# Neighbourhood bias loaded as one laid-out tensor, a new order of loads and splits in the conditioning, and a mixer without the two long reciprocals

## The reference

```
sh_a, sc_a, g_a, sh_f, sc_f, g_f = split(silu(c) @ w_ada + b_ada)     # the same for c_ctx
h, hc   = rms(x) * (1 + sc_a) + sh_a, rms(ctx) * (1 + csc_a) + csh_a
q, k, v, u, vs = h @ w_in;   kc, vc = hc @ w_in[:, 512:1536]          # q, k normalised per head
s_win   = q . k_window * scale + rpb[head, key row - row + 7, key column - column + 15]
s       = concat(s_win, q . kc * scale);  o = softmax(s) @ (v_window, vc)
x       = x + g_a * (concat(rms(o), rms(sgu(u, vs))) * gain) @ w_out
x       = x + g_f * mixture_of_experts(x)
```

```
r, i    = sigmoid(gates of xb)
log_a   = 8 * r * log_sigmoid(lam);   a = exp(log_a)
mult    = sqrt(-expm1(2 * log_a))                                     # = sqrt(1 - a * a)
h_t     = a_t * h_(t-1) + mult_t * (i_t * xb_t)
p       = softmax(concat(scores + band bias, sink))                   # a head's row
```

## Time and profile before

| | |
|---|---|
| median of 3 runs (2688.72 to 2693.19) | 2691.13 us |
| the profiled execution: its own time | 2688.06 us |
| the profiled execution: its span | 2685.8 us |
| PE busy, share of the span | 2486.6 us, 93% |
| DVE, ACT, POOL busy | 53%, 38%, 4% |
| mean granted clock of PE | 0.968 |
| conditioning | 0 to 46 us |
| projection | 46 to 220 us |
| heads of the first mixer, from the first maxima | 1247.6 to 1299.2 us |
| heads of the second mixer | 2199.6 to 2254.4 us |

### The profile page before, as it was taken

One profiled execution on the slowest core, in us unless ns is written; L12 is line 12 of the kernel. 1 busy time (PEld: TensorE's weight loads), 2 busy tenths in 40 slices (PEclk: granted clock), 3 DMA queues, 4 the chain that ended last, 5 costly groups with the idle time before them and its releaser, 6 DMA issues. The chain is left out here.

```text
span 2685.8 us, 33498 instructions
## 1 busy us (share of the span) xinstructions
PE 2486.6 (93%) x12262; PEld 2056.9 (77%) x12262; DVE 1428.8 (53%) x2063; ACT 1014.8 (38%) x1466; POOL 98.2 (4%) x115
## 2 busy tenths in 40 slices
PE   6887877999969999997899999999999987999998
PEld 3765856888768888785798888888888856988886
DVE  4676667999843332487653332523323777633324
ACT  5325535777722232244433222322222345322221
POOL 0241001000010000000000000000000000000000
PEclk8997988999979999999999999999999998999999
DMA  5974278999752333240233332423323312323322
GB/s 220 320 262 157 89 282 291 409 403 404 313 180 79 101 94 94 86 113 32 63 98 98 94 97 94 122 72 95 100 94 102 90 55 63 95 78 95 100 94 71
DMA packets 313412, 389.55 MB, mean 145 GB/s; under 512 B 15530, under 2 KB 228170, under 8 KB 313316
## 3 DMA queue, kind: packets, MB, share of 16 engines
q1 hardware_dynamic: 301272, 346.15, 38.8%
q0 software_dynamic: 9024, 33.03, 3.4%
q10 hardware_dynamic: 3020, 9.07, 0.8%
HBM read 354.04 MB, written 41.96 MB: 147 GB/s over the span
## 5 line engine op out<-in xcount | busy, mean ns | idle before, releaser
L1652 DVE TENSOR_TENSOR w_part_lo<-w_raw,w_part_hi 128x1024 fp32r<-128x1024 f32 x252 | 308.3, 1225 | 734.0 <-ACT w_part_hi L1648 733.3
L1656 PE MATMUL PS<-xT_hi,w_part_hi 128*128 128x512 f32 (+1 forms) x1472 | 555.9, 378 | 17.5 <-PEq L1924 8.3
L1648 ACT ACTIVATE w_part_hi<-w_raw 128x1024 fp32r<-128x1024 f32 x252 | 266.5, 1060 | 789.8 <-PE PS L1658 755.2
L1657 PE MATMUL PS<-xT_lo,w_part_hi 128*128 128x512 f32 (+1 forms) x1472 | 554.3, 377 | 0.0
L1658 PE MATMUL PS<-xT_hi,w_part_lo 128*128 128x512 f32 (+1 forms) x1472 | 554.1, 376 | 0.0
L1656 PEld LDWEIGHTS PS<-xT_hi,w_part_hi 128*128 128x128 f32 x1472 | 279.0, 190 | 71.1 <-DVE w_part_lo L1652 19.9
L1658 PEld LDWEIGHTS PS<-xT_hi,w_part_lo 128*128 128x128 f32 x1472 | 278.9, 189 | 50.3
L1657 PEld LDWEIGHTS PS<-xT_lo,w_part_hi 128*128 128x128 f32 x1472 | 279.1, 190 | 49.2
L1656 PE MATMUL PS<-w_part_hi,h_hi 128*128 128x512 f32 x576 | 228.2, 396 | 0.0
L1657 PE MATMUL PS<-w_part_lo,h_hi 128*128 128x512 f32 x576 | 227.9, 396 | 0.0
L1658 PE MATMUL PS<-w_part_hi,h_lo 128*128 128x512 f32 x576 | 227.9, 396 | 0.0
(11 more groups left out here) (479 smaller groups left out, 4116.6 us busy)
## 6 DMA issues: line engine op xcount, KB each, us to landing
expert_w_raw<-in_w SPq DMA_DIRECT2D x136, 512.0 KB, 7.2
w_raw<-in_ffn_w_gate SPq DMA_DIRECT2D x88, 512.0 KB, 3.8
w_raw<-in_ffn_w_up SPq DMA_DIRECT2D x88, 512.0 KB, 3.9
w_raw<-in_ffn_w_down SPq DMA_DIRECT2D x88, 512.0 KB, 3.8
w_raw<-in_w SPq DMA_DIRECT2D x68, 512.0 KB, 6.4
w_raw<-in_w_in SPq DMA_DIRECT2D x56, 512.0 KB, 5.4
late_raw<-in_w_ada SPq DMA_DIRECT2D x32, 512.0 KB, 11.5
w_raw<-in_w_out SPq DMA_DIRECT2D x24, 512.0 KB, 5.0
```

What stands on the lines that cost most here:

```text
L1648: nc.scalar.activation(t.hi, raw[t.n % 4], ACT.Copy).then_inc(w_hi, 1)
L1652: nc.vector.tensor_tensor(t.lo, raw[t.n % 4], t.hi.bitcast(f32), ALU.subtract).then_inc(w_lo, 1)
L1656: nc.tensor.matmul(out, a[0][a_at], b[0][b_at], start=first, stop=False, skip_group_check=True)
L1657: nc.tensor.matmul(out, a[0][a_at], b[1][b_at], start=False, stop=False, skip_group_check=True)
```

## The change

1. The bias table comes in as a tensor `rpb_windows`, laid out by query and key outside the kernel, and one DMA of 3 MB on POOL's queue loads it into `nbt`, after the second group's result is out of PSUM. The padded rows, the shifted copies and the 24 reads are gone. The 8 additions of the mask stay.
2. In the conditioning the first 2 MB of `w_ada` are loaded ahead of x. ACT's scaling of x moves behind the first two pieces, and PE's early transposes behind the fourth.
3. Tiles 0 and 1 of `w_in` are split at the end of the conditioning instead of the start of the projection.
4. PE's first product waits for two chunks of x instead of four, and goes block by block.
5. In the mixer, mult is made from a: ACT squares a, DVE makes (a² + 1) tanh(t) in one instruction in head 1, and ACT takes its square root next to the one of the convolution's norm. 1 - a² equals (1 + a²) tanh(t), with a = exp(-t). The scan, the product with the gate and the last split of the recurrence each stand one head earlier. POOL has one product left.
6. The sink's part of the row maximum: a copy and one TENSOR_SCALAR a head are gone from DVE; ACT's exponential adds the sink as its bias.

```diff
@@ -226,8 +222,9 @@
         @block.sync
         def _(sp):
             sp.dma_start(c2[:, :, :], A["cT"]).then_inc(s_c, 16)
-            sp.dma_start(xtok[:, :, :], A["x"][0].rearrange("(b p) d -> p b d", p=P)).then_inc(s_x, 16)
             for i, (q0, q1) in enumerate(ADA_LOADS):
+                if i == 1:
+                    sp.dma_start(xtok[:, :, :], A["x"][0].rearrange("(b p) d -> p b d", p=P)).then_inc(s_x, 16)
                 sec, k0 = q0 // KC, q0 % KC
                 sp.dma_start(wada[:, q0:q1, :], A["w_ada"][0, k0 * P:(k0 + q1 - q0) * P, sec * D:(sec + 1) * D].rearrange("(k p) n -> p k n", p=P)).then_inc(s_aw[i], 16)
...
+            act.dma_start(out_gT[:, :], A["out_gainT"]).then_inc(s_in, 16)
...
             nc.scalar.activation(ssum[:, 0:TB], ssum[:, 0:TB], ACT.Sqrt, bias=eps6[:, 0:1], scale=1.0 / D).then_inc(s_rt, 1)
-            act.wait_ge(s_rpb, 16)
-            act.dma_start(rpad_rows.rearrange("h (r w) -> (h r) w", w=RP), rpad[:, :]).then_inc(s_rpr, 16)
-            act.wait_ge(s_rt, 2)
-            for b in range(2):
-                nc.scalar.activation(xn[:, b, :], xtok[:, b, :], ACT.Copy, scale=ssum[:, b:b + 1]).then_inc(s_xn, 1)
             for q in pieces:
                 p = q - WHOLE
+                if p == 2:
+                    act.wait_ge(s_rt, 2)
+                    for b in range(2):
+                        nc.scalar.activation(xn[:, b, :], xtok[:, b, :], ACT.Copy, scale=ssum[:, b:b + 1]).then_inc(s_xn, 1)
                 act.wait_ge(s_aw[load_of(q)], 16)
                 if p >= 4:
                     act.wait_ge(a_used, p - 3)
                 nc.scalar.activation(a_whi[:, p % 4, :], wada[:, q, :], ACT.Copy).then_inc(a_hi, 1)
                 if q == KC + 1:
                     rows_out(0)
+            split_hi(Tile(0))
+            split_hi(Tile(1))
             rows_out(1)
...
+            split_lo(Tile(0))
+            split_lo(Tile(1))
...
                     nc.tensor.matmul(PS[0:4, rows_bank[0] + h, :], sc4[:, q, :], wada[:, q, h * HALF:(h + 1) * HALF], start=q == 0, stop=False, skip_group_check=True)
-            pe.wait_ge(s_xn, TB)
-            pe.wait_ge(s_in, 48)
-            for c in EARLY:
-                for b in range(TB):
-                    nc.tensor.transpose(PS[:, c, b * P:(b + 1) * P], xn[:, b, c * P:(c + 1) * P], ident[:, :])
...
+                if q == KC - 1:
+                    pe.wait_ge(s_xn, TB)
+                    pe.wait_ge(s_in, 48)
+                    for c in EARLY:
+                        for b in range(TB):
+                            nc.tensor.transpose(PS[:, c, b * P:(b + 1) * P], xn[:, b, c * P:(c + 1) * P], ident[:, :])
...
-            for h in range(8):
-                each = bass.AP(rpad_rows.tensor, h * NDR * RP, [[0, NB_ROWS], [0, QCOLS], [1, NDR * RP]])
...
-            for h in range(8):
-                for kind, off in enumerate((0, -8, -16)):
-                    skew = bass.AP(skewed.tensor, h * (P + 1) * SKEW + 7 * RP + GRID - 1 + off, [[SKEW, P], [RP, NB_ROWS], [1, WCOLS]])
-                    pool.dma_start(nbt[:, h, kind * WIN:(kind + 1) * WIN].rearrange("p (k c) -> p k c", c=WCOLS), skew).then_inc(s_tab, 16)
+            pool.wait_ge(evac1, 2)
+            pool.dma_start(nbt[:, :, :], A["rpb_windows"]).then_inc(s_tab, 16)
...
-            pool.wait_ge(s_tab, 16 * 25)
+            pool.wait_ge(s_tab, 32)
...
-            pe.wait_ge(rd1, 4)
...
                 src, nb = (XT, TB) if g < NCOL else (HC, CB_)
-                for kk in range(2):
-                    kc = 2 * kp + kk
-                    for b in range(nb):
+                for b in range(nb):
+                    if n == 0 and b >= 2:
+                        pe.wait_ge(rd1, b + 1)
+                    for kk in range(2):
+                        kc = 2 * kp + kk
...
-                    pool.drain()
-                    nc.gpsimd.tensor_scalar(i_g[:, :, :], th[:, :, :], 1.0, None, ALU.add).then_inc(m["divisor"], 1)
+                    pool.wait_ge(m["gates_out"], l + 1)
+                    nc.gpsimd.tensor_tensor(xc[:, :, :], xc[:, :, :], i_g[:, :, :], ALU.mult).then_inc(m["gated_in"], 1)
...
-                    last.then_inc(m["tanh_out"], 1)
+                        nc.scalar.activation(sig[:, ch, :], r_g[:, ch, :], ACT.Exp, scale=lamc[:, ch, 6:7])
+                    act.drain()
+                    nc.scalar.activation(r_g[:, :, :], sig[:, :, :], ACT.Square).then_inc(m["tanh_out"], 1)
...
-                            nc.scalar.activation(esink[:, u % 4, :], smax[:, u % 2, :], ACT.Exp)
+                            nc.scalar.activation(esink[:, u % 4, :], nmax[:, u % 2, :], ACT.Exp, bias=sink_l[:, u:u + 1])
...
-                        if u == 3:
-                            act.wait_ge(m["mult_sq"], l + 1)
-                            nc.scalar.activation(th[:, :, :], th[:, :, :], ACT.Sqrt).then_inc(m["mult_out"], 1)
                         if u == 2:
                             act.wait_ge(m["var_done"], l + 1)
                             nc.scalar.activation(xb[:, 0, 0:SEQ], PS[:, 7, :], ACT.Sqrt, bias=eps[:, 0:1]).then_inc(m["std_out"], 1)
...
+                        if u == 2:
+                            act.wait_ge(m["mult_sq"], l + 1)
+                            nc.scalar.activation(th[:, :, :], th[:, :, :], ACT.Sqrt).then_inc(m["mult_out"], 1)
+                        if u == 5:
                             act.wait_ge(m["scan_out"], l + 1)
...
-                        V.tensor_copy(row_sink[:, u % 2:u % 2 + 1], sink_l[:, u:u + 1])
...
-                        V.tensor_scalar(nmax[:, u % 2, :], mx, row_sink[:, u % 2:u % 2 + 1], -1.0, ALU.max, ALU.mult)
-                        dve.drain()
-                        V.tensor_scalar(mx, nmax[:, u % 2, :], row_sink[:, u % 2:u % 2 + 1], None, ALU.add)
+                        V.tensor_scalar(nmax[:, u % 2, :], mx, sink_l[:, u:u + 1], -1.0, ALU.max, ALU.mult)
...
-                            dve.wait_ge(m["divisor"], l + 1)
-                            V.reciprocal(i_g[:, 0, :], i_g[:, 0, :])
-                        elif u == 2:
-                            V.reciprocal(i_g[:, 1, :], i_g[:, 1, :])
-                            dve.drain()
-                            V.scalar_tensor_tensor(th[:, :, :], th[:, :, :], 2.0, i_g[:, :, :], ALU.mult, ALU.mult).then_inc(m["mult_sq"], 1)
-                        elif u == 4:
+                            dve.wait_ge(m["tanh_out"], l + 1)
+                            V.scalar_tensor_tensor(th[:, :, :], r_g[:, :, :], 1.0, th[:, :, :], ALU.add, ALU.mult).then_inc(m["mult_sq"], 1)
+                        elif u == 3:
                             dve.wait_ge(m["mult_out"], l + 1)
+                            dve.wait_ge(m["gated_in"], l + 1)
                             V.tensor_tensor(xc[:, :, :], xc[:, :, :], th[:, :, :], ALU.mult)
                             dve.drain()
                             for ch in range(2):
                                 V.tensor_tensor_scan(th[:, ch, :], sig[:, ch, :], xc[:, ch, :], 0.0, ALU.mult, ALU.add)
                             dve.drain()
-                        elif u == 5:
+                        elif u == 4:
                             V.tensor_tensor(xc[:, :, :], th[:, :, :], gb[:, :, :], ALU.mult).then_inc(m["scan_out"], 1)
-                        elif u == 7:
+                        elif u == 6:
                             dve.wait_ge(m["y_hi"], l * 5 + 1)
...
+    A["rpb_windows"] = c(np.stack([rows[:, 7 + kr - qr, GRID - 1 + off + kc - qc].reshape(8, P, WIN) for off in (0, -8, -16)], 2).transpose(1, 0, 2, 3).reshape(P, 8, 3 * WIN))
```

30 lines of the change are left out of this document (7 added, 23 removed).

## The result

The changed kernel takes 2661.51 us (median of 4 runs, 2659.99 to 2665.99) against 2692.16 us of the kernel before in the same comparison (4 runs, 2688.72 to 2693.23). The ratio, worked out over all of these runs, is 0.9891, with a 95% interval of 0.9874 to 0.9908: 29 us or 1.1% less (the two medians lie 30.7 us apart). The forecast was 2661, from a sum of 28.6.

What follows compares the result with a forecast made beforehand. PE was taken to bound most of the program, with gains only where it waits. Terms 17 + 4.6 + 7 = 28.6 us gave 2659.5 from the profiled execution, 2662.5 from the median, stated as 2661; range from one below 2649 to 2676.

Steps and rivals of the forecast that it cites:

- the exchange of the loads: Conditioning: w_ada's first 2 MB ahead of x starts PE's whole products 5.2 us sooner, but only 0.4 us comes through.
- The projection, -17: Projection: without the bias copies' DMA traffic, 17 us of the 19.6 us lost waiting for weight tiles come back.
- the 2.7 us left for POOL's additions: Projection: POOL's 8 mask additions still slow DVE's work beside them, so 2.7 us of the loss stays.
- The loss of 19.6: Projection: the stretch of 16 tiles takes 112.5 us against 92.9 undisturbed, so 19.6 us are lost.
- The start, -4.6: Conditioning and head of the projection: load order 0.4, earlier splits 1.9, fewer chunks 2.3, in sum 4.6 us; bounds 2 and 6.
- the splits 1.89 (forecast 1.9): Head of the projection: splitting tiles 0 and 1 earlier takes ACT's 2.01 us away there, of which 1.9 count.
- the chunks 2.28 (2.3): Projection's first product: waiting for two chunks of x instead of four lets it start about 2.3 us sooner.
- The mixers, -3.5 each: Two mixers' heads: less DVE work gains 4.0 us, ACT's square takes part back; 3.5 us each, 7 in all.
- The first (mixers gain nothing): Mixers: ACT sets the pace and its square delays every exponential, so nothing is gained; 2668 or 2670 us, chance 0.15.
- the fourth (the stall is the weights' own): Projection: its own weights and late loads cause the stall, so few of the 17 us come; 2677.5 us, chance 0.05.
- The second: Projection: the bias load starves the weights for a tile, 5.45 us, and PE's clock falls; 2666.5 us, chance 0.12.
- the third: Mixers and projection: heads gain 6 us a layer, projection loses nothing and its clock is 1.00; 2649 us, chance 0.15.
- the fifth: Behind the projection: PE pauses less and gets the lower clock more often, so the kernel is slower; chance 0.03.

Runs made afterwards that it cites:

- run 5: The changed kernel with POOL's eight mask additions spread out, one in each tile's time instead of two; 2655.56 us, 0.9869 of before.
- run 8: The changed kernel with x loaded ahead of the first half section of w_ada again, all else kept; 2659.79 us, 0.9886 of before.
- run 12: The changed kernel with additions spread, x first, distance-row loads earlier, ACT's square behind head 0's exponentials, recurrence ahead of head 3's division; 2656.86 us, 0.9871 of before.
- run 6: The changed kernel with the old sink's copy and second TENSOR_SCALAR of each head back on DVE; 2668.47 us, 0.9909 of before.
- run 7: The changed kernel with the mixer's root, recurrence, gate product and last split in their old heads, new formula and sink kept; 2661.55 us, 0.9883 of before.
- run 3: The kernel before with the mixer's change alone; 2685.20 us, 0.9971 of before.
- run 1: The kernel before with the bias change alone, one load in place of padded rows, copies and 24 reads; 2677.31 us, 0.9938 of before.
- run 9: The changed kernel with the bias table load allowed as soon as the last transposes are done; 2663.95 us, 0.9892 of before.

## Why the prediction was right

Its sum was 28.6 and 29 were measured (24.8 to 33.9). Each term can be checked, and the nearness of the sum is in part luck: for the projection it had up to 1.6 us too much, for the exchange of the loads 0.4 that did not come, and the mixers gave a little more.

**The projection, -17 (bounds 11 to 19.7).** Right in mechanism and nearly in size: 15.35 in the changed kernel's trace and 17.0 in that of the bias alone, whose measured time fell by 16.7. The late bias load (99.99, forecast some 97) did not make PE wait. The mis-sized piece is the 2.7 us left for POOL's additions: they cost 3.3 where the clock held and 4.9 where PE's wait of 2.6 us had a lower clock behind it, which I had not priced. The loss of 19.6 was itself 0.7 too small, as a late row adds 1.73 us and not 1.88 and the undisturbed length is 92.26; the two errors partly cancel. Spread out, the additions cost nothing (run 5).

**The start, -4.6.** The first product came 4.05 us sooner. Two of three steps hold to 0.1 us up to there: the splits 1.89 (forecast 1.9), the chunks 2.28 (2.3). The third, "of the 5.2 us only 0.4 comes through" for the exchange of the loads, is wrong in sign: nothing came through, and with x first the conditioning ends some 2 us sooner (run 8, 2.66 in the single pair of traces). I had ACT's chain on x right, but took the pieces to begin "about when they did" (they begin at 20.26, and with x first at 19.3 to 19.9), and didn't ask what PE's gap between the whole products and the pieces does to its clock. The moved scaling and transposes made up for this loss: with x first, where only they and the earlier splits differ, the conditioning ends some 1.8 us sooner than in the kernel before. I had given them nothing.

**The mixers, -3.5 each.** The numbers of the walk held: head 4 at the old place, the end 3.3 earlier against 3.5. That head 4 hit the old place is partly luck. I let the recurrence wait for ACT's root, until 1269.9 on the old scale. The root was done 1.2 us sooner (1252.05 + 16.65 = 1268.70), and the recurrence waited for the division ahead of it, which I had left out; with the division behind it (run 12) head 4 starts 1.5 us sooner. The measured 7.8 for both mixers fits the 7 of the sum too, though part of it is the clock that the old heads lost more often. The shares inside differ as well: I gave the sink's instructions 1.55 of the 3.5, and run 6 took 2.9 and 2.5 us for them, most of it at a lower clock. My claim that the moved recurrence eats the gain of heads 1 and 2 before head 4 was right, and run 7 adds that it eats it at any place. The saved table loads were slack, as counted. By the Trainium skill (ScalarE: Activation LUTs, "What ACT_TABLE_LOAD costs") each of them frees 2.66 us of ACT, by the rows 1.28. Run 7 with two loads more is no slower, so its time can't tell them apart, but the rows do: before and behind the loads at 1266.90 and at 1249.12 ACT's timeline has no gap of more than 0.03 us, and in run 7 ACT is busy for 2.7 us more over a mixer's heads, two loads of 1.28. Here the load alone is the cost.

**The rivals.** The first (mixers gain nothing) falls with run 3, and the fourth (the stall is the weights' own) with run 1. The second is real as a mechanism (run 9) and without a price. That the weights yield to the large load is also what the Trainium skill's rule would make of it, by which engines drain a whole packet before they switch (DMA: Bandwidth & Descriptors, "Queues, rings and completion order"). The trace of the changed kernel agrees: from 99 to 114 us POOL's queue moved 3.15 MB in 144 packets and took 51.6% of the engines' time, the other 2.22 MB in 860 packets and 39.6%. Run 9's wait of 6.8 us fits it, without showing the packets. Of the third, the heads gave more than 3.5 a mixer only where the old ones had lost clock, and not because DVE leads; a projection without loss and at a clock of 1.00 came only with the additions spread, and then the time was 2655.56. For the fifth, the mean clock was 0.969 against 0.968: it did not fall.

What stays open: in the profiled pair the experts' stage, from PE's first transposes of the experts' rows (L1404 in the changed kernel) to the first gather of their results on POOL (L1835), took 3.5 us longer after the change (331.8 against 328.3), which no part of the change touches. The two windows at its beginning, of before and of after:

```profile
430.00:480.00 50.00, 44.31 (x206) 35.67 (x205) 41.12 (x38) 35.90 (x39) 0.00 (x0) 1.00 0.95 349
```

```profile
410.00:460.00 50.00, 44.10 (x191) 35.40 (x190) 37.78 (x36) 33.37 (x36) 0.00 (x0) 0.93 0.87 325
```

The granted clock is 1.00 in one and 0.93 in the other at the same 44 us of busy time. Over all fourteen traces the stage took 328.3 to 333.6 us, in the three with the old mixer 328.3 to 329.5 and in the eleven with the new one 329.5 to 333.6. The mixer stands behind this stage; whether that is chance or a shift of when the clock falls was not tried.
